# Third gated stage of a hybrid network: the output products as three split passes

## The reference, cut to what matters

```
h = rms_norm(x, pre_mix_g); z = h @ w_in
o_a = hgrn2_mixer(...); o_b = gla_mixer(b_q, b_k, b_v, b_code, b_g, ...)
o_c = mla_mixer(...);   o_d = gdn_mixer(...)
mix = concatenate([o_a, o_b, o_c, o_d]) @ w_out
x = x + rms_norm(mix, post_mix_g)            # then the ffn in the same manner
```

## Time and profile before

| what | value |
|---|---|
| median of three runs | 2261.98 us (2260.5 to 2272.67) |
| the profiled execution | 2270.98 us, its span 2269.2 us |
| PE busy | 2146.0 us, 95% of the span |
| DVE busy | 1243.4 us, 55% |
| ACT busy | 921.9 us, 41% |
| plain products L753 on output tiles (`oT`) | 208 records, 109.6 us |

### The profile page before, as it was taken

The page is one execution under the profiler, slowest core; times in us unless marked ns, Lnnn a source line. Parts: engine busy times, 40 slices in busy tenths (PEclk is TensorE's granted clock), DMA queues, the critical chain, the costliest instruction groups (busy, mean ns, idle before and its releaser), DMA issues. The chain is left out here.

```text
span 2269.2 us, 35816 instructions
## 1 busy us (share of the span) xinstructions
PE 2146.0 (95%) x14692; PEld 1585.3 (70%) x14692; DVE 1243.4 (55%) x2133; ACT 921.9 (41%) x1665; POOL 45.6 (2%) x36
## 2 busy tenths in 40 slices
PE   7999999899999999999989999998999988999998
PEld 4786644688888777765447888886877566887546
DVE  5655444766662375473456666524538774444554
ACT  5424434433332354153344333323346553423552
POOL 2000001000000020000010000000000000000000
PEclk9999999999999999999999999999999999999999
DMA  5201111122222221020112223222321102222001
GB/s 200 75 3 57 57 39 38 58 109 93 93 93 105 82 75 56 22 76 20 57 38 75 93 96 109 93 75 97 109 80 56 38 22 90 93 93 88 25 1 38
DMA packets 23922, 159.82 MB, mean 70 GB/s; under 512 B 3024, under 2 KB 3664, under 8 KB 4944
## 3 DMA queue, kind: packets, MB, share of 16 engines
q1 hardware_dynamic: 23760, 157.53, 19.5%
HBM read 155.43 MB, written 2.10 MB: 69 GB/s over the span
## 5 line engine op out<-in xcount | busy, mean ns | idle before, releaser
L678 DVE TENSOR_TENSOR arena_r<-ring,arena_r 128x512 fp32r<-128x512 f32 x486 | 337.1, 704 | 462.0 <-ACT arena_r L669 458.8
L669 ACT ACTIVATE arena_r<-ring 128x512 fp32r<-128x512 f32 x486 | 299.3, 628 | 597.6 <-PE banks L719 566.1
L717 PE MATMUL banks<-oT_r,arena_r 128*128 128x512 f32 x1136 | 465.3, 410 | 14.1 <-DVE arena_r L678 9.0
L719 PE MATMUL banks<-oT_r,arena_r 128*128 128x512 f32 x1136 | 445.7, 392 | 0.0
L718 PE MATMUL banks<-hT_r,arena_r 128*128 128x512 f32 x1008 | 395.4, 392 | 0.0
L717 PE MATMUL banks<-arena_r,arena_r 128*128 128x512 f32 x712 | 290.6, 408 | 17.5 <-DVE arena_r L709 10.7
L718 PE MATMUL banks<-arena_r,arena_r 128*128 128x512 f32 x744 | 292.3, 393 | 0.0
L719 PE MATMUL banks<-arena_r,arena_r 128*128 128x512 f32 x712 | 279.3, 392 | 0.0
L717 PEld LDWEIGHTS banks<-oT_r,arena_r 128*128 128x128 f32 x1136 | 215.4, 190 | 74.5 <-DVE arena_r L955 12.4
L719 PEld LDWEIGHTS banks<-oT_r,arena_r 128*128 128x128 f32 x1136 | 215.1, 189 | 46.0
L718 PEld LDWEIGHTS banks<-hT_r,arena_r 128*128 128x128 f32 x1008 | 190.9, 189 | 44.6 <-issue 7.9
(11 more groups left out here) (394 smaller groups left out, 2935.0 us busy)
## 6 DMA issues: line engine op xcount, KB each, us to landing
ring<-weights SPq DMA_DIRECT2D x142, 1024.0 KB, 4.8
xT<-x_features SPq DMA_DIRECT2D x2, 1024.0 KB, 6.4
arena<-memory SPq DMA_DIRECT2D x2, 1024.0 KB, 5.0
y_features<-xT SPq DMA_DIRECT2D x8, 256.0 KB, 2.0
const<-constants SPq DMA_DIRECT2D x1, 1088.0 KB, 15.9
const<-constants SPq DMA_DIRECT2D x1, 512.0 KB, 16.7
arena<-positions SPq DMA_DIRECT2D x1, 256.0 KB, 2.4
small<-small_vectors SPq DMA_DIRECT2D x2, 68.5 KB, 6.6
```

The source lines that it names most:

```text
L669: act.activation(hi, self.stream.block(b, n), ACT.Copy).then_inc(self.chip.sem("hi_ready"), 1)
L678: vec.tensor_tensor(lo[:, 0:n * P], self.stream.block(b, n), hi[:, 0:n * P].bitcast(F32), ALU.subtract).then_inc(self.chip.sem("lo_ready"), 1)
L717: pe.matmul(out, w_hi, hi, start=k == 0, stop=False)
L719: ins = pe.matmul(out, w_lo, hi, start=False, stop=k == nk - 1)
```

## The change

In group 2 the first unit of `outad` stays plain and the seven others, 28 products, are made split. The four inputs are split into the tiles 41 to 48, and seven chunks of weights, one per unit, into seven pairs of tiles of their own. Three unused blocks are put ahead of `outad` and three taken away behind the units `uk`, so that a unit of four blocks is a chunk. The counts of `GLA_RUNS[2]` change: 31 of the 32 products lie in 12 runs, of which two hold the plain ones (29 in 15 runs before), and the rest at the end. On ACT the splits stand in the order: four inputs and two chunks ahead of LF_HI; one chunk behind it and behind the first unit's result; four chunks behind the key copy, ahead of the late exponentials. On DVE: four inputs and one chunk ahead of LF_LO, two chunks behind the first selection, four behind QM, ahead of the late weights. ACT takes four units' results instead of three behind the late exponentials.

More of the change, by code:

```diff
@@ L115, in layer_plan @@
     p.unit("gk", "gla_w_gk2", 1, cols(0), rows=16)
+    p.blocks += 3 * [None]
     out_part(p, "outad", (0, 1, 6, 7))
@@ L1590, in gla_stage @@
     else:
-        parts, first, more, early = None, [], [], 0
+        parts = lambda k: (chip.t_r(41 + k), chip.t_r(45 + k))
+        first, more = [(33, 34), (35, 36), (37, 38), (12, 49), (50, 51), (52, 53), (54, 55)], []
+        early = 1
     source = chip.h if group == 0 else None if group == 1 else lambda k: chip.o((0, 1, 6, 7)[k])
@@ L1595, in gla_stage @@
     whole = GLA_WHOLE[group]
[L1596 to L1600, removed]
+    pairs = lambda tiles: [(chip.t_r(i), chip.t_r(j)) for i, j in tiles]
+    split = Split(chip, stream, g0 + whole, u1, pairs(first), head=pairs(more), whole=g0 + whole - u0,
+                  given=1 if group == 1 else 0, ahead=SPLIT_BLOCKS if group == 0 else 0)
     meanwhile = Meanwhile(chip, stream, g0, u1, evac, source, split, whole, parts)
@@ L1757, in _ @@
                 act.activation(V_TOK[:, :, 2 * j:2 * j + 2, :], bank, ACT.Copy).then_inc(chip.sem("t_used"), 1)
-            if group != 1 and split:
+            if group != 1:
                 for i in range(KD if hgrn else 4):
@@ L1773, in _ @@
                 split.scalar_chunks(act, 4)
-            if not hgrn and not split:
+            if group == 2:
                 meanwhile.scalar(act, 1)
+                split.scalar_chunks(act, 3)
             def exponentials(first, half):
@@ L1790, in _ @@
                 split.scalar_chunks(act, 6)
+            if group == 2:
+                split.scalar_chunks(act, 7)
             exponentials(E_LATE, 0)
@@ L1793, in _ @@
                 split.scalar_chunks(act, 7)
-            meanwhile.scalar(act, 2 if hgrn else 3)
+            meanwhile.scalar(act, 2 if hgrn else 4)
             for h in range(left):
@@ L1855, in _ @@
                     lo_part(chip, vec, i, source(i), *parts(i))
-            elif split:
+            elif group == 1:
                 split.vector_chunks(vec, len(split.chunks))
+            else:
+                split.vector_chunks(vec, 3)
             vec.wait_ge(chip.sem("t_used"), E_EARLY + 4)
@@ L1871, in _ @@
                 free(stt(QM[h], q, chip.c(masks)[:, h:h + 1], D[:, QE], ALU.mult, ALU.mult))
-            if group == 0:
-                split.vector_chunks(vec, 6)
+            if group != 1:
+                split.vector_chunks(vec, 6 if hgrn else 7)
             vec.wait_ge(chip.sem("t_used"), E_LATE + 4)
```

17 lines of the change are left out of this document (6 added, 11 removed).

## The result

The changed kernel takes 2272.28 us (median of 20 runs, 2267.38 to 2278.2), the kernel before 2265.93 us (20 runs, 2259.96 to 2272.67; the three runs shown at first had a median of 2261.98). The ratio is 1.0028, 95% interval 1.0019 to 1.0037: slower by some 6 us. The profiled execution is a run of 2277.01 us, near the slow end of its twenty, with a span of 2275.2 us, 6.0 us above the one before.

A forecast was written before the change was run, and what follows sets the result against it. PE was taken as the bound, busy 2146.0 of 2269.2 us. 4.0 us gained in both layers less 3.4 for the clock left 0.6 off the median 2261.98: 2261.4, say 2261, range 2254 to 2268.

The forecast's parts named there:

- The products: On PE: 28 split products at 0.73 us instead of 0.88 save 4.2 us per layer, 8.4 us in both, as ceiling.
- The splits' copies: Per layer 11 new copies on ACT (5.9 us) and 11 subtractions on DVE (6.6 us), judged to fit; place decides.
- the first wait of 0.5 us: Layer 0, near 283: PE waits about 0.5 us for the first split weights.
- the lead of 2.0 us: Layer 1, late decays: 1.3 us earlier as in layer 0, plus some 0.7 us from its longer half-clock start.
- The new wait: In front of the second diagonal: PE's wait for DVE's unchanged chain grows from 0.49 us to 2.3 (2.0 to 2.5).
- The clock: Behind the diagonal's wait: a short half-clock drop in each layer, costing 3.4 us together, bounds 0 and 6.8.
- rival B: Half clock's long form behind the diagonal's waits and the stage's end: 10.2 us against 4.0, +6, 2268; chance 0.13.
- The rule against it: Skill page: matmul streams broken up by waits are throttled again and again, so the drop comes each time; no size.
- The idle stretch at 2059 us: Elsewhere in the earlier profile: after 2.72 us of idling the clock stayed at 1.00, so the drop need not come.
- The end of the stage: The norm's chain, 4.44 us, now ends the stage, where PE's last three products outlasted it: 0.45 us more per layer.
- The base: Whole kernel: the forecast difference was carried to the runs' median of 2261.98 us.

The follow-up runs named there:

- e6: Changed kernel plus two thrown-away products at the stage's end, cutting PE's boundary wait from 2.66 us to 0.96: 2265.68 us, ratio 1.0001 to the kernel before.
- e14: Changed kernel with one plain unit kept, two products moved in front of the second diagonal and three left behind the norm: 2263.96 us, ratio 0.9983 to the kernel before.
- e2: Kernel before with only the output blocks shifted by three places, nothing else: 2265.57 us, ratio 0.9994 to the kernel before.
- e1: Changed kernel plus two thrown-away products in front of the second diagonal and two behind the last product: 2264.25 us, ratio 0.9985 to the kernel before.
- e3: Changed kernel with the run counts of before, so the splits alone: 2272.46 us, ratio 1.0031 to the kernel before.
- e7: Changed kernel with the stage's two loads held until the units using their slots are done, as before: 2274.24 us, ratio 1.0049 to the kernel before.
- e9: Changed kernel with the last run count 0 instead of 2, leaving three products behind the norm: 2270.97 us, ratio 1.0007 to the kernel before.
- e12: Kernel before plus one thrown-away product per layer in the 1.21 us boundary wait: 2265.16 us, ratio 0.9980 to the kernel before.
- e5: Changed kernel plus two thrown-away products in front of the second diagonal only: 2273.53 us, ratio 1.0039 to the kernel before.
- e13: Changed kernel with two plain units instead of one, its own run counts kept: 2270.80 us, ratio 1.0012 to the kernel before.
- e8: Changed kernel with two plain units, two more products in front of the second diagonal and three behind the norm: 2258.34 us, ratio 0.9967 to the kernel before.

## Why the prediction was wrong

The forecast was 2261, no change, range 2254 to 2268; the kernel takes 2272.28 and is slower by 0.28%. In difference to before, -0.6 us was forecast and +6.35 us measured.

- **The products.** Right. Runs of four split products took 2.86 us (287.15 to 290.01), 0.72 us each, forecast 0.73.
- **The splits' copies.** Right in layer 0: their place, their hiding in DVE's holes, ACT's late exponentials and the first wait of 0.5 us. Layer 1 was forecast 0.7 us better than layer 0, because it starts at half clock for longer. Where it did start so, that came true: in layer 1 of e6 and e14, which are the changed kernel up to there, the late decays come 19.1 and 19.2 us behind the stage's first product, where before it was 21.1 (1053.74 to 1074.83), with the same 6.8 us of half clock at the start. That is the lead of 2.0 us (1.3 + 0.7) that I had at this point. But in the changed kernel's profile layer 1 started at full clock. PE then came to the first split weights 2.00 us too early, half clock followed, and the late decays came at 19.8 us. The kernel before with the new layout (e2), whose layer 1 also started at full clock, has them at 17.8: there the splits do not win 2.0 us, they lose 2.0. The first split product starts 8.8 us behind the stage's first one in layer 1 of e1, e3, e7 and e9 too, whether PE waited 2.00, 0.74 or 0.33 us for it. This dependence on the clock at the start, which is one draw, was not in the forecast. With the 1.05 us wait for issue it left a gain at full clock of about 2.3 us for both layers instead of 4.0.
- **The new wait.** Right in place and releaser, 1.80 us for 2.3.
- **The clock: the step that failed.** "I take a short drop in each layer: 3.4 us, bounds 0 and 6.8." This term of the sum was too small. Over all executions the changed kernel has 17 us more of half clock than the kernel before, worth 7 to 9 us where 3.4 were charged. Half of the 17 us is up to 8.7, and less the gain of 2.3 above that makes +6.4, where +6.35 was measured. The price of a half-clock stretch was right (a half of its length; e6 and e12 against the changed kernel show it). Its places were not counted in full. I charged the wait in front of the diagonal alone and left the longer wait at the boundary for rival B, at 0.13; the 2.00 us wait for split weights in layer 1 I had not foreseen. e6 fills the boundary's wait and wins back all 6.6 us, e5 fills the diagonal's alone and wins nothing, and e3 has half clock and the whole loss by waits inside the stage.
- **Rival B,** at 2268, has the right mechanism and nearly the right sum: 10.2 us of price against 4.0 of gain, +6. Both of its terms are too high by some 1.5 us, and that these cancel is luck.
- **The rule against it.** The page of the Trainium skill that was cited, "TensorE: Matmul & The Clock Gate", section "HAM oscillation — how this bites in real kernels", spoke against this change, and the change was slower. It is not the same case, though: that section tells of waits of about 3 to 5 us for DMA, and here waits of 2.5 to 2.7 us were followed by half clock each time and waits of 1.2 to 1.3 us in half of the cases. The idle stretch at 2059 us without a drop, which I put beside it, was one draw.
- **The end of the stage.** Right in the sum: from the norm's first product to the boundary 5.22 us follow from the forecast (5.67 us before, less 0.45) and 5.23 were measured. What I did not see is that it need not be so. The new counts moved two products ahead of the norm and so delayed the norm's chain by 1.5 us; e9 leaves them behind it and has a ratio lower by 0.0021.
- **The base.** 2261.98 was the median of three runs; over 20 it is 2265.93. 4 us of the miss of 11 are this.
- **What stays open.** The four stretches account for 3.0 us of the 6.0 between the two profiles (237.7 against 234.7 us, each taken to the next stage's first product). The rest lies outside, in code that did not change, where the changed kernel's profile had 11 us more of half clock (73 against 62); one profile of each can't say whether that is chance. Filling the boundary's wait won 1 to 3 us more than the saved half clock accounts for (e1, e6), and filling the diagonal's saved none; neither is explained. The wait for "issue" among the state updates in layer 1 (1.05 us in the changed kernel and in e14, about 1 us in e1, e5, e6 and e7, none in e9 and e13) isn't explained either; the stage's second load is excluded. In five of these six cases half clock begins within 0.3 us of its end.

## What to carry to other kernels

Faster filler work is worth nothing where the filler only covers another engine's chain: move the counts until the covered waits are as short as before, or keep part of it slow (e8 did both). Keep enough independent work to follow the last small products of a stage; PE's idle time at a barrier can be paid for twice, once as the wait and once as half clock in the stage behind, if that one is bound by PE. Before pricing a change at a few us, look at the scatter of the baseline. Where the clock is in question, compare the mean granted clock of all executions, which one profile can't replace.

## What the runs showed of the hardware

Useless matmuls can make a kernel faster: e12 differs from the kernel before by two products of about 0.86 us in all its 2266 and is 0.20% (0.06 to 0.34) faster. I had not expected that a boundary wait of 1.2 us, which the kernel before already had, could be worth filling.

How often a wait was followed by half clock went with its length. At the boundary, a stretch of half clock began between 0.4 us before and 2.3 us after PE's next product:

| boundary wait | boundaries in all profiles | followed by half clock | half clock in the stage behind, mean us |
|---|---|---|---|
| 2.5 to 2.7 us | 12 | 12 | 10.1 |
| 1.2 to 1.3 us | 12 | 6 | 8.5 |
| 0.57 to 0.96 us | 8 | 0 | 3.0 |

The last column holds more than what follows the wait: in 26 of the 32 cases another stretch of half clock begins 24 to 34 us behind the boundary, inside the stage behind. In front of the diagonal, waits of 1.2 to 2.4 us were followed by half clock in 10 of 11 cases, waits of 0.3 to 1.1 us in none of 13; the 2.00 us waits for split weights in 5 of 5. The single wait in front of the diagonal alone won nothing by being filled (e5), and why is not shown.
